# The norm of x taken from its rows, nine small vectors on another queue, conv flips moved, wide first-pair products, and last evictions on two engines, in a one-layer decoder step on one core

## The reference, cut to what matters

```python
h = rms_norm(x, w['g_norm1']) * (1 + sc1) + sh1      # x * rsqrt(mean(x*x) + EPS) * g
proj = h @ w['w_in']                                 # q | k | v | forget | z | xBC | dt | gate A | gate B
q = rms_norm(q, g_q); k = rms_norm(k, g_k)           # per head
# branch A: forgetting attention; branch B: Mamba-2, with a causal convolution over xBC
# whose last 3 rows (conv_new) are an output, and whose first 3 come from state_conv
x = x + gt1 * (m @ w['w_o'])
h2 = rms_norm(x, w['g_norm2']) * (1 + sc2) + sh2
x = x + gt2 * grouped_moe(h2, ...)                   # 16 experts, two for each row
```

## Time and profile before

| | us |
|---|---|
| three runs | 812.23, 816.81, 812.26 |
| median | 812.26 |
| the profiled execution | 817.01 |
| its span, first to last instruction | 815.4 |
| mean granted clock in it | 0.976 |

### The profile page before, as it was taken

The page is one execution under the profiler, slowest core; times in us unless marked ns, Lnnn a source line. Parts: engine busy times, 40 slices in busy tenths (PEclk is TensorE's granted clock), DMA queues, the critical chain, the costliest instruction groups (busy, mean ns, idle before and its releaser), DMA issues.

```text
span 815.4 us, 12570 instructions
## 1 busy us (share of the span) xinstructions
PE 772.4 (95%) x4601; PEld 538.8 (66%) x4601; DVE 366.0 (45%) x847; ACT 294.6 (36%) x731; POOL 94.2 (12%) x155
## 2 busy tenths in 40 slices
PE   3798999999998999999988999999999999999987
PEld 2575687778785777888877788888744444444434
DVE  2455457777772275687997201113221313121213
ACT  1213237666772235659863001012312212211213
POOL 3321011122101115221001000000010000000000
PEclk9999999999999999999999989999599999999999
DMA  9797456879866522369997974373699999999992
GB/s 285 240 355 220 154 171 172 284 246 308 272 236 207 160 62 62 104 177 398 336 287 274 335 316 156 104 264 138 229 351 419 422 420 422 421 421 421 421 415 81
DMA packets 93387, 219.47 MB, mean 269 GB/s; under 512 B 11697, under 2 KB 67577, under 8 KB 78836
## 3 DMA queue, kind: packets, MB, share of 16 engines
q1 hardware_dynamic: 78850, 181.71, 61.4%
q0 software_dynamic: 7840, 31.67, 11.8%
q10 hardware_dynamic: 6634, 5.25, 2.1%
HBM read 207.05 MB, written 13.22 MB: 270 GB/s over the span
## 4 chain that ended last, share of the span: by engine, by line
PE 64%; DMA 10%; SPq 8%; ACT 7%; DVE 5%; issue 3%; ACTq 1%; POOLq 1%; POOL 0%; DVEq 0%
PE bank L1643 14%; PE bank L1977 8%; SPq L559 8%; PE bank L1871 7%; DMA out_ssm_sample<-arena 4%; PE bank L1576 4%; PE bank L2001 4%; PE bank L1639 4%; PE bank L1879 4%; DMA arena<-in_w_down 3%; PE bank L1853 3%; PE bank L1597 2%; PE bank L2020 2%; DMA arena<-in_conv_w 2%; PE bank L1948 1%
## 5 line engine op out<-in xcount | busy, mean ns | idle before, releaser
L1643 PE MATMUL bank<-h_normed,weight_ring 128*128 128x264 f32 x1024 | 238.9, 390 | 2.0 <-ACT conv_work L1006 2.0
L1643 PEld LDWEIGHTS bank<-h_normed,weight_ring 128*128 128x128 f32 x1024 | 192.5, 191 | 37.7 <-issue 3.5
L1977 PE MATMUL bank<-arena,h_normed 128*64 128x512 f32 x176 | 79.5, 604 | 0.0
L1871 PE MATMUL bank<-y_T,weight_ring 128*128 128x264 f32 x256 | 60.0, 399 | 0.1
L1977 PE MATMUL bank<-weight_ring,h_normed 128*64 128x512 f32 x192 | 56.6, 594 | 0.7 <-DMA arena<-in_w_up 0.7
L1871 PEld LDWEIGHTS bank<-y_T,weight_ring 128*128 128x128 f32 x256 | 50.3, 197 | 9.3 <-issue 0.2
L1507 DVE SCALAR_TENSOR_TENSOR x_residual<-bank,modulation,x_residual 128x256 f32<-128x256 f32 x64 | 28.8, 484 | 58.4 <-PE bank L2020 58.4
L1500 DVE TENSOR_TENSOR arena<-arena,bank 128x512 f32<-128x512 f32 x8 | 8.5, 1056 | 99.3 <-PE bank L1977 99.3
L1576 PE MATMUL bank<-identity,arena 128*128 128x128 f32 (+5 forms) x236 | 32.4, 279 | 16.1 <-ACT arena L841 9.2
L1576 PEld LDWEIGHTS bank<-identity,arena 128*128 128x128 f32 (+5 forms) x236 | 27.1, 150 | 26.7 <-issue 12.3
L998 ACT ACTIVATE arena<-conv_out,expanded 128x128 f32<-128x128 f32 x128 | 38.3, 387 | 13.9 <-DVE arena L1383 12.9
(11 more groups left out here) (364 smaller groups left out, 1195.4 us busy)
## 6 DMA issues: line engine op xcount, KB each, us to landing
weight_ring<-in_w_in SPq DMA_DIRECT2D x36, 1024.0 KB, 6.3
weight_ring<-in_w_mod SPq DMA_DIRECT2D x22, 1024.0 KB, 9.8
arena<-in_w_up SPq DMA_DIRECT2D x14, 1024.0 KB, 22.6
weight_ring<-in_w_gate SPq DMA_DIRECT2D x14, 1024.0 KB, 21.1
arena<-in_w_down SPq DMA_DIRECT2D x11, 1024.0 KB, 26.2
weight_ring<-in_w_up SPq DMA_DIRECT2D x10, 1024.0 KB, 19.5
arena<-in_state_ssm POOLq DMA_DIRECT2D x8, 1024.0 KB, 9.2
out_ssm_sample<-arena POOLq DMA_DIRECT2D x8, 1024.0 KB, 9.8
```

Source lines behind the costliest of these rows:

```text
L1643: ins = mm(ps[:, 0:T], w, hT[:, c, :], start=c == 0, stop=c == KD - 1)
L1871: ins = mm(ps[:, 0:T], w, yT[:, c, :], start=c == 0, stop=c == NXB - 1)
L1977: ins = mm(banks[i][BLK * e:BLK * e + BLK, :], xg[:, 4 * h + c, BLK * e:BLK * e + BLK], ws[e][:, c, :], start=h == 0 and c == 0, stop=h == ...
```

## The change

- **Norm of x.** The squares come from the rows: ACT squares each of three blocks of `xin` with a running sum (`accum_out`), takes the roots, DVE the reciprocals and three diagonal matrices, and `ssq` spreads them by three products of ones with a diagonal, now behind `("mod", 1)`. DVE's eight squares are gone; ACT's root over [128, 264] becomes a copy.
- **Loads.** The nine small vectors go from SP's queue to ACT's, behind the SiLU of c, on `head_in`; the router's weights stay on SP, four pieces of w_in later, on `router_in`. `csin` is loaded as 96 partitions of 3 KB and flipped in 3 + 3 flips instead of 12 + 12; the two `cst` jobs stand right before `fd`, and DVE's copies of them have three strided parts.
- **Keys.** `("q", 1)` stands between `ft` and the norms of k.
- **Tails.** `ct` 0, 1 and 2 move out of `fill` to before `sp`, between `so` 0 and `sx` 0, and between `so` 1 and `sx` 1. `ctok` has two places.
- **First pair.** `gather(h)` is three products with `sel` as the stationary side and 512 columns of `h2tok` moving, into banks 0 and 1 as rows; DVE copies each bank to `xrow`, and `turn` flips them as for the later pairs. `first_wts` comes behind the turns; DVE does the choice weights behind the two copies, and `select(r, 1)` no longer waits for `xf_filled`.
- **End.** ACT copies `late` 0, 2, 4 and DVE 1, 3, 5, behind its `If`.
- Some semaphores are shared now (`rows_out`).

```diff
@@ views
+        xsq = u[:].rearrange("p c t -> p (c t)")[:, 0:D]
+        rdiag = u[:].rearrange("p c t -> p (c t)")[:, D:D + 384].rearrange("p (a t) -> p a t", a=3)
-        csin = ar[:, D:D + CD]
+        csin = ar[0:96, D:D + CD // 4]
-        ctok = cw[:, 2 * XW:2 * XW + 512]
+        ctok = (cw[:, 2 * XW:2 * XW + 512], cw[:, 0:512])
@@ jobs
-        jobs += [("vecs",), ("ssq", 0), ("mod", 1), ("modt", 1), ("cst", 0), ("cst", 1), ("mod", 0), ("modt", 0), ("fd",)]
-        jobs += [("k", i) for i in range(4)] + [("q", 0)] + [("ft",)] + [("kn", i) for i in range(4)]
-        jobs += [("q", i) for i in range(1, 5)] + [("qn", i) for i in range(4)]
+        jobs += [("vecs",), ("mod", 1), ("ssq", 0), ("modt", 1), ("mod", 0), ("modt", 0), ("cst", 0), ("cst", 1), ("fd",)]
+        jobs += [("k", i) for i in range(4)] + [("q", 0), ("ft",), ("q", 1)] + [("kn", i) for i in range(4)]
+        jobs += [("q", i) for i in range(2, 5)] + [("qn", i) for i in range(4)]
...
-                jobs += [("sm",), ("mod", 5), ("sp",), ("modt", 5)]
+                jobs += [("sm",), ("mod", 5), ("ct", 0), ("sp",), ("modt", 5)]
-        jobs += [("so", 0), ("sx", 0)] + [("z", i) for i in range(4)] + [("so", 1), ("sx", 1)]
+        jobs += [("so", 0), ("ct", 1), ("sx", 0)] + [("z", i) for i in range(4)] + [("so", 1), ("ct", 2), ("sx", 1)]
-        fill = {(0, 1): [("z", 4)], (0, 2): [("ct", 0)], (0, 3): [("z", 5)], (0, 4): [("ct", 1)],
-                (0, 5): [("z", 6), ("ct", 2)], (0, 6): [("ct", 3)], (0, 7): [("z", 7)], (1, 0): [("z", 8), ("zs", 0)],
+        fill = {(0, 1): [("z", 4)], (0, 3): [("z", 5)], 
+                (0, 5): [("z", 6)], (0, 6): [("ct", 3)], (0, 7): [("z", 7)], (1, 0): [("z", 8), ("zs", 0)],
@@ SP
-                sp.dma_start(wr[:], t["w_router"].rearrange("(k p) e -> p k e", p=128)).then_inc(late_in, 16)
-                for h in range(2):
-                    sp.dma_start(gqk[64 * h:64 * h + 64, 0:1], t["g_q"].rearrange("o d -> d o")).then_inc(late_in, 16)
...
+                if s == loads[loads.index(("in", COL_K)) + 4]:
+                    sp.dma_start(wr[:], t["w_router"].rearrange("(k p) e -> p k e", p=128)).then_inc(router_in, 16)
@@ ACT
-            act.dma_start(csin[0:24, :], t["state_conv"].rearrange("o b w c -> (o b w) c")).then_inc(st_in, 16)
+            act.dma_start(csin, t["state_conv"].rearrange("o b w (q c) -> (o b w q) c", q=4)).then_inc(st_in, 16)
             act.dma_start(pgs[:], t["page_table"].rearrange("(o b) g -> o (b g)", o=1)).then_inc(pt_in, 16)
             act.wait_ge(cond_in, 32)
             link(fn(crow[0:NC, :], crow[0:NC, :], ACT.Silu), cond_ready)
+            for h in range(2):
+                act.dma_start(gqk[64 * h:64 * h + 64, 0:1], t["g_q"].rearrange("o d -> d o")).then_inc(head_in, 16)
...
+            act.wait_ge(x_in, 48)
+            act.wait_ge(consts, 3)
+            for a, (t0, n) in enumerate(TOK):
+                link(fn(xsq[0:n, :], xin[0:n, a, :], ACT.Square, accum_out=sm2[0:n, a:a + 1]))
+            link(fn(sm2[:, 4:6], sm2[:, 0:2], ACT.Sqrt, bias=epsc[:], scale=1.0 / D), sq_ready)
+            link(fn(sm2[0:NS, 6:7], sm2[0:NS, 2:3], ACT.Sqrt, bias=epsc[0:NS], scale=1.0 / D), sq_ready)
-                for j in late:
+                for j in late[0::2]:
@@ DVE
-                        for c in range(KD):
-                            square(c)
+                        dve.wait_ge(sq_ready, 2)
+                        link(v.reciprocal(sm2[:, 8:10], sm2[:, 4:6]))
+                        link(v.reciprocal(sm2[0:NS, 10:11], sm2[0:NS, 6:7]))
+                        for b, (t0, n) in enumerate(TOK):
+                            v.tensor_scalar(rdiag[0:n, b, 0:n], ident[0:n, 0:n], sm2[0:n, 8 + b:9 + b], None, ALU.mult)\
+                             .then_inc(rd_ready, 1)
@@ DVE, round_of
                 if first:
+                    for h in range(2):
+                        dve.wait_ge(rows_summed, h + 1)
+                        v.tensor_copy(xrow[:, 512 * h:512 * h + 512], banks[h][:]).then_inc(rows_copied, 1)
                     choice_weights()
                 weights_of(r, 0)
-                if first:
-                    dve.wait_ge(xf_filled, 3)
                 select(r, 1)
+            for j in late[1::2]:
+                ps, (a, f), n = filled(dve, j), j[1:], TOK[j[1]][1]
+                release(dve, v.tensor_copy(yout[0:n, a, 512 * f:512 * f + 512], ps[0:n, :]), j)
@@ PE
-                    for c in range(KD):
-                        pe.wait_ge(sq_ready, c + 1)
-                        ins = mm(ps[:, 0:T], onesf[:], u[:, c, :], start=c == 0, stop=c == KD - 1)
+                    for a, (t0, n) in enumerate(TOK):
+                        pe.wait_ge(rd_ready, a + 1)
+                        ins = mm(ps[:, t0:t0 + n], onesf[0:n, :], rdiag[0:n, a, 0:n], start=True, stop=True)
@@ PE, gather(h)
-                    for q in range(4):
-                        c = 4 * h + q
-                        ins = mm(banks[5 + h][:, 128 * q:128 * q + 128], h2tok[a][0:n, 128 * c:128 * c + 128], sel[0:n, a, :],
-                                 start=q == 0 and a == 0, stop=a == 2, skip_group_check=True)
-                ins.then_inc(xf_filled, 1)
+                    ins = mm(banks[h][:], sel[0:n, a, :], h2tok[a][0:n, 512 * h:512 * h + 512], start=a == 0, stop=a == 2)
+                ins.then_inc(rows_summed, 1)
@@ PE, round_of
                 if first:
                     gather(0)
-                    pe.wait_ge(tokw_ready, 1)
-                first_wts(r)
-                if first:
                     gather(1)
                 else:
-                    turn(r, 0, 0)
-                    turn(r, 0, 1)
+                    first_wts(r)
+                turn(r, 0, 0, first)
+                turn(r, 0, 1, first)
+                if first:
+                    pe.wait_ge(tokw_ready, 1)
+                    first_wts(r)
+                else:
                     ids(r, 1)
```

More of the change, by code:

```diff
@@ L868, in _ @@
                 elif k == "ssq":
-                    act.wait_ge(consts, 3)
-                    release(act, fn(rs[:, 0, :], ps[:, 0:T], ACT.Sqrt, bias=epsc[:], scale=1.0 / D), j)
+                    release(act, fn(rs[:, 0, :], ps[:, 0:T], ACT.Copy), j)
                 elif k == "fd":
@@ L1806, in _ @@
                 elif k == "sw":
+                    pe.wait_ge(router_in, 16)
+                    pe.wait_ge(head_in, 16 * 9)
                     for c in range(KD):
@@ L1899, in _ @@
             shifted_at = [bank_of[("hx", 2, f)][0] for f in range(2)]
-            assert 5 not in shifted_at and 6 not in shifted_at
+            assert not {0, 1, 5, 6} & set(shifted_at), shifted_at
             for b in range(NBANK):
@@ L1970, in gate_up @@
                         pe.wait_ge(samp_read, it * 8 + 1)
+                    if first:
+                        pe.wait_ge(rows_copied, i + 1)
                     for h in range(2):
```

85 lines of the change are left out of this document (43 added, 42 removed).

## The result

The changed kernel's median is 807.93 us (802.05 to 814.66, 14 runs), that of the kernel before beside it 812.64 us (809.03 to 817.78, 14 runs). The time lies above the range's upper end, 806.5. The profiled execution of the changed kernel took 807.14 us, near its median, while the one of the kernel before took 817.01, 4.4 above its own. So the two traces differ by 9.8 us of span (815.4 to 805.6) and the runs by 4.7. Both differences need an account, and the first reading can only give the larger one.

What follows compares the result with a forecast made beforehand. PE bounds the kernel until `gate_half`, then full DMA at 421 GB/s sets the end, `gate_half` plus 194 us plus a tail. Terms 4.5 + 4.2 + 1.1 + 3.6 + 0.7 = 14.1, less 2.1: gain 12.0, 800.3 us; range 796.5 to 806.5.

Steps and rivals of the forecast that it cites:

- all at half clock: First pair, old gather: 5.72 us for its first half, `first_wts`, as much again, gate product from 589.19, at half clock.
- Start, 4.5 forecast: Up to `fd`: first products on `("mod", 0)` end 2.0 us earlier, small-vector wait 1.7 gone, clock 0.8; bounds 1 and 7.
- the idle gap gets shorter; I take 0.8: Around `fd`: half clock from 39.4 to 42.8 us costs up to 1.7; 0.8 us credited as gain.
- Keys, 4.2: Keys: `("q", 1)` fills PE's 2.5 us wait, half clock costing 1.7 goes; gain 4.2 us, bounds 1.5 and 4.4.
- It just holds: Keys: DVE's chain behind the last `kn`, about 10.1 us, fits under PE's three q blocks, 10.8 us.
- Tails, 1.1: Scan stage: three `ct` leaving save 1.8 us, 0.5 and 0.2 given back; gain 1.1, bounds -0.5 and 1.9.
- First pair, 3.6: First pair: wide sums bring `gate_half` to 590.8 from 594.4 us, gain 3.6; loss 1.2 at half clock, 6.5 at best.
- A sign that the prediction had named for being wrong: First pair: the prediction is wrong if the gate product starts at half clock after an idle stretch.
- the first pair gives nothing: Rival, first pair: low clock stays through the wide sums or returns before the gate product; 803.9 us, chance 0.2.
- Its joint case: That rival together with a start giving only what SP's issues hid: 806.9 us and up, chance 0.05.
- End, 0.7: Last evictions: two engines cut the 0.8 us or so behind PE's last flip to one copy; bounds -1 and 0.9.
- The baseline: Whole kernel: profiled run 4.75 us above the median may hold half-clock losses the median lacks; 2.1 us taken off.

## Why the prediction was wrong

Forecast were 12.0 us, 4.7 came. The step that failed most is the price of the old gather in the first pair, "all at half clock"; next to it the 0.8 us of clock at the start, the 1.7 at the keys and the term of the end.

- **Start, 4.5 forecast.** The mechanism was right, and its signs came (`fd`'s end at 40.2, where 39.7 was named, the landing, over 300 GB/s): the load's shape, its 225 GB/s, the landing (2.1 us against 1.5 taken), the small wait. In the trace `fd` came 4.0 us earlier. But "the idle gap gets shorter; I take 0.8" has the wrong sign: freed PE time became waits for landings, and the low clock around `fd` grew to as much as 13.7 us. Mean of the profiles: 43.8 to 41.5, 2.3 us. Here the size failed, by the price of the clock.
- **Keys, 4.2.** Mis-sized: 1.4 at full clock, 3.1 where it falls. "It just holds" failed by 0.9 us, since the chain behind the last `kn` also has a table load of 1.28 us that had been hidden by the wait that the edit took away. And 1.7 of the 4.2 is there only where the clock falls, in two of three profiles of before.
- **Tails, 1.1.** The scan stage gave 1.5, about as taken. Ahead of `so` 0 the copy and stores cost 0.5 to 0.8 (taken: 0.5) and now and then the clock. The net can't be told from nothing.
- **First pair, 3.6.** This is the step of the prediction that failed most: "all at half clock" as a property of the old gather. It is so in four of eight profiles; in the others the narrow stage took 12.2 or 14.0 us, not 18.2. The trace's gain, 4.0 us, looks like a hit and is mostly the comparison of a bad draw with a good one. At equal clock the wide form is 1.7 to 1.9 us slower, by the serial chain that I had put at 3.1 and had not set against a narrow form at full clock. For the wide form the forecast of 14.5 us was near the 14.1 measured, but by two errors that cancel: the sums took 5.9 us for 7.1, and the first half of the gate product 5.3 for 4.3. A sign that the prediction had named for being wrong was there too: the clock fell at the gate product (578.0 to 581.4 us), behind two short waits. In all ten wide profiles it fell between 0.9 us before that product's start and 0.2 us after it. The rival that had this right, "the first pair gives nothing", stood at 0.2 and gave 803.9. Its joint case with a start that gives less, at 0.05 and "806.9 and up", is nearest to what came. The prediction says that its range takes in most of that case; but the case starts at 806.9, above the range's end of 806.5.
- **End, 0.7.** Wrong: the "one copy" to which two engines would take the tail was not what the end waited for. SP's six stores set it. They gained nothing from earlier copies; the second could be issued 1.67 us behind the first eviction's start, where with ScalarE alone it was issued at 1.25.
- **The baseline.** I took 2.1 us off for a profiled execution 4.75 us above the median. The further profiles put all of it where my terms had credited it: 1.7 at the keys and 4 to 6 in the first pair, in the executions that draw the low clock there, and nothing in the others. With the excess of 4.75 taken off, the sum of 14.1 would have given 9.4 us, still twice what came.

Together, on the means of the profiles: start 2.3, keys 2.5 (55.2 to 52.7), first pair 1.6 (16.2 in the three profiles of before, 14.6 wide), end -1.8 (7.1 to 8.9 in the eight profiles with wide sums and the alternation; its cause is open), tails about 0. That is 4.6, against 4.7 and 4.2 us between medians. So close a match is partly luck: with the mean of all eight narrow profiles, 15.6, the first pair gives 1.0 instead of 1.6.

## What to carry to other kernels

When a profiled execution is slower than the median, take the excess out of the very terms that touch its low-clock stretches, or profile the kernel again first: the same instructions took 12.2 us in one execution and 18.2 in another here. When an edit removes a wait, look for what was hidden under it (a table load, a queue's issues) and add that to the chain that must now fit. PE time freed in front of a landing is worth only as much as the landing moves.

## What the runs showed that I had not expected

- A load of 288 KB as 24 partitions of 12 KB took the traffic of its neighbours from 320 to 239 GB/s (in all) for 5 us and delayed the last weight piece by 2.2 us; as 96 partitions of 3 KB it did not.
- The low clock over the same instructions of the first pair lasted 3.4, 6.8 or 17.1 us from one execution to the next, and PE was busy throughout the 17.1.
- Six float32 sums of 512 columns and twelve with 128 columns, over the same data, took 3.1 and 3.2 us at full clock.
- Among SP's last six stores one issue took about 1.3 us in nearly every profile, and in some a second one as long; the cause is open.
